# Dilated attention layer: rotary embedding moved from VectorE to GpSimd, and the first head's keys turned beside the memory queries

## What is computed

```python
DIL_GROUPS = ((128, 1), (512, 4), (2048, 16))
DIL_HEADS, DIL_HEAD_DIM, ROPE_DIM = 6, 128, 32

def partial_rope(x, pos):            # the first 32 of a head's 128 features
    half = ROPE_DIM // 2
    ...
    x1, x2 = xr[..., :half], xr[..., half:]
    rot = jnp.concatenate([x1 * cos - x2 * sin, x1 * sin + x2 * cos], axis=-1)
    return jnp.concatenate([rot, x[..., ROPE_DIM:]], axis=-1)

def dilated_mixer(h, w_in):
    for g, (window, dil) in enumerate(DIL_GROUPS):
        qkv = (h @ w_in[:, base:base + 3 * MIXER_WIDTH]).reshape(B, T, 3, DIL_HEADS, DIL_HEAD_DIM)
        q = partial_rope(qkv[:, :, 0], pos)
        k = partial_rope(qkv[:, :, 1], pos)
        o, lse = dilated_group(q, k, qkv[:, :, 2], window, dil)
    ...
    rest = h @ w_in[:, len(DIL_GROUPS) * 3 * MIXER_WIDTH:]
    q_mem, gate = jnp.split(rest, [MEM_WIDTH], axis=-1)
```

## Time and profile before

| | us |
|---|---|
| median of 3 runs | 3156.7 (3155.58 to 3156.95) |
| the profiled execution | 3151.94 |
| its span in the trace | 3150.6 |
| PE busy | 2860.4 (91%) |
| DVE busy | 1624.0 (52%) |
| ACT busy | 1019.8 (32%) |
| POOL busy | 182.2 (6%) |

### The profile page before, as it was taken

How to read it: one execution, slowest core, us unless ns; L and a number is a source line. 1 busy time by engine, 2 the same in 40 slices (tenths; PEclk the granted TensorE clock), 3 DMA queues, 4 the chain that set the end, 5 groups by cost and what they waited for, 6 DMA issues and landing times.

```text
span 3150.6 us, 43505 instructions
## 1 busy us (share of the span) xinstructions
PE 2860.4 (91%) x18290; PEld 2322.3 (74%) x18290; DVE 1624.0 (52%) x3099; ACT 1019.8 (32%) x1974; POOL 182.2 (6%) x258
## 2 busy tenths in 40 slices
PE   8988879999999988899699999999899897899998
PEld 6767667877776666688567888888666686578886
DVE  4333535544436455767864424343935677654444
ACT  3223422222234245343243212122425444332222
POOL 0000000000000000100000000000201244000001
PEclk9999989999999999899899999999999898899999
DMA  6433332232222210223522121121121110223231
GB/s 231 160 109 136 108 86 50 70 79 61 66 107 94 62 34 1 71 80 97 175 80 94 41 81 59 62 67 54 54 59 34 33 39 1 94 94 111 90 106 55
DMA packets 228878, 250.95 MB, mean 80 GB/s; under 512 B 6048, under 2 KB 193548, under 8 KB 227404
## 3 DMA queue, kind: packets, MB, share of 16 engines
q1 hardware_dynamic: 227008, 243.87, 24.4%
q0 software_dynamic: 1344, 4.20, 0.6%
q10 hardware_dynamic: 332, 0.12, 0.0%
HBM read 234.53 MB, written 9.44 MB: 77 GB/s over the span
## 4 chain that ended last, share of the span: by engine, by line
PE 68%; DVE 12%; ACT 4%; issue 2%; DMA 1%; POOL 0%; SPq 0%; DVEq 0%; ACTq 0%; POOLq 0%
PE PS L2235 63%; PE PS L2239 3%; ACT AR L182 1%; ACT L177 1%; DMA WR<-in_w_in 1%; PE PS L2424 1%; PE PS L2446 1%; DVE AR L3227 1%; DVE STAT L3159 1%; DVE AR L3066 1%; ACT EX L182 1%; DVE AR L3064 0%; DVE EX L3214 0%; DVE AR L2962 0%; ACT STAT L182 0%
## 5 line engine op out<-in xcount | busy, mean ns | idle before, releaser
L2235 PE MATMUL PS<-HI,WC 128*128 128x512 f32 (+2 forms) x1600 | 428.0, 353 | 0.7 <-DVE WC L3208 0.7
L2235 PE MATMUL PS<-AR 128*64 128x64 f32 (+7 forms) x3436 | 305.2, 269 | 64.0 <-ACT AR L182 27.2
L2235 PEld LDWEIGHTS PS<-AR 128*64 128x64 f32 (+5 forms) x3436 | 258.5, 171 | 116.4 <-issue 37.2
L182 ACT ACTIVATE AR<-PS 128x512 f32<-128x512 f32 (+5 forms) x353 | 152.1, 457 | 545.0 <-PE PS L2235 410.6
L2235 PEld LDWEIGHTS PS<-HI,WC 128*128 128x128 f32 x1600 | 284.0, 189 | 42.5 <-DVE WC L3208 1.1
L2235 PE MATMUL PS<-LO,WC 128*128 128x512 f32 (+2 forms) x800 | 282.2, 353 | 0.0
L2235 PE MATMUL PS<-HT,WR 128*128 128x256 f32 (+1 forms) x928 | 260.9, 434 | 6.0 <-DMA WR<-in_w_in 2.6
L2235 PE MATMUL PS<-WR,HT 128*128 128x128 f32 (+2 forms) x1296 | 251.6, 352 | 12.0 <-ACT AR L182 5.0
L182 ACT ACTIVATE EX<-PS 128x256 f32<-128x256 f32 (+2 forms) x158 | 66.6, 430 | 532.6 <-PE PS L2235 532.5
L2235 PEld LDWEIGHTS PS<-WR,HT 128*128 128x128 f32 x1296 | 191.7, 197 | 62.7 <-issue 39.1
L2235 PE MATMUL PS<-WC,AC 128*128 128x512 f32 x960 | 227.1, 393 | 0.3
(11 more groups left out here) (461 smaller groups left out, 5173.0 us busy)
## 6 DMA issues: line engine op xcount, KB each, us to landing
WR<-in_w_ffn_in SPq DMA_DIRECT2D x40, 1024.0 KB, 7.1
WR<-in_w_in_b SPq DMA_DIRECT2D x51, 512.0 KB, 6.8
WR<-in_w_mod SPq DMA_DIRECT2D x12, 2048.0 KB, 7.9
WR<-in_w_mod SPq DMA_DIRECT2D x24, 1024.0 KB, 5.6
WR<-in_w_ffn_out SPq DMA_DIRECT2D x22, 1024.0 KB, 4.9
WR<-in_w_in SPq DMA_DIRECT2D x40, 512.0 KB, 5.2
WR<-in_w_out SPq DMA_DIRECT2D x8, 2048.0 KB, 10.8
WR<-in_w_in SPq DMA_DIRECT2D x4, 2048.0 KB, 7.9
```

Source lines behind the costliest of these rows:

```text
L182: return self.o.activation(out, in_, func, **kw)
L2235: mm = lambda o, l, r, start, stop: e.o.matmul(o, l, r, start=start, stop=stop, skip_group_check=True)
```

## The change

All three operations of the rotary step go from DVE to POOL (`rope_d` becomes `rope_g`, with the same waits and the same semaphore), for all 12 steps. `rope_s` stays on POOL. For head 0 the keys' `rope_s` is still added at the end of `head_project(0)`, but their `rope_g` is held over in `owed_rope` and added in `memory_queries()`, after the work of f = 0; `qk_done[0]` is set there. Heads 1 to 5 keep their places in the plan.

```diff
         def memory_queries():
             owed_made()
             w = parts[3]
             parts_load(4, spill_done)
+            late, made = owed_rope[0]
...
                 for j in (2 * f, 2 * f + 1):
                     parts_made(4, j)
+                if f == 0:
+                    made += rope(*late)
+                    qk_done[0] = latest(made)
...
         def rope(x, copied):
 
-            if P.count["rope_s"] == P.count["rope_d"]:
+            if P.count["rope_s"] == P.count["rope_g"]:
                 P.add("rope_s", x, copied)
                 return []
-            return [("rope_d", 2 * P.add("rope_d", x, copied))]
+            return [("rope_d", 2 * P.add("rope_g", x, copied))]
...
-            for _ in late:
-                done += rope(*late)
+            if h == 0:
+                rope(*late)
+                owed_rope.append((late, done))
+                return
             qk_done[h] = latest(done)
```

More of the change, by code:

```diff
@@ L1361, in more_parts @@
                 high_made(p, step - 3)
-        owed_parts = []
+        owed_parts, owed_rope = [], []
         def owed_made():
@@ L3056, in rope @@
                 tt(x2, r4[2], r4[3], ALU.add).then_inc(sem(name))
[L3058 to L3068, removed]
             def rope_a(n, sg, rt, i, ready, until):
@@ L3229, in dve_program @@
             return dict(setup=setup, setup2=setup2, fence=fence, norm1=norm1, norm2=norm2, pj1=pj1, pjc=pjc, ma_x=ma_x, ma_t=ma_t, ma_f=ma_f, ga=ga, turn=turn_, mod_0=mod_0, mod_d=mod_d,
-                        gl=gl, hp1=hp1, hp2=hp2, hp5=hp5, hl1=hl1, hl2=hl2, hl4=hl4, hoe=hoe, rj=rj, gz=gz, g1=g1, g2=g2, g4=g4, g5=g5, g7=g7, rope_d=rope_d, rope_a=rope_a, qturn=qturn,
+                        gl=gl, hp1=hp1, hp2=hp2, hp5=hp5, hl1=hl1, hl2=hl2, hl4=hl4, hoe=hoe, rj=rj, gz=gz, g1=g1, g2=g2, g4=g4, g5=g5, g7=g7, rope_a=rope_a, qturn=qturn,
                         da_x=da_x, da_t=da_t, da_o=da_o, fnorm=fnorm, rr_c=rr_c, rg=rg, rr=rr, cols=cols, an=an, rs=rs, df_x=df_x, df_w=df_w, df_o=df_o, df_q=df_q,
@@ L3289, in rope_s @@
                     e.o.dma_start(w[lo:lo + 16, :, :], x[16 - lo:32 - lo, :, :]).then_inc(sem("rope_dm"), 16)
+            def rope_g(n, x, copied):
+                u, w = (a[0:32, :].rearrange("p (g n) -> p g n", g=3) for a in RTs)
+                cc, ss = (RC[0:32, 512 * c:512 * c + 512].unsqueeze(1).broadcast_to([32, 3, 512]) for c in range(2))
+                e.wait_all(copied)
+                e.wait_ge("tables", 80)
+                e.wait_ge("rope_d", 2 * n - 2)
+                tt(u, x, cc, ALU.mult)
+                e.wait_ge("rope_dm", 32 * n)
+                tt(w, w, ss, ALU.mult).then_inc(sem("rope_d"))
+                e.wait_ge("rope_d", 2 * n - 1)
+                tt(x, u, w, ALU.add).then_inc(sem("rope_d"))
             def swap(n, to, src, need):
@@ L3293, in swap @@
                 e.o.dma_start(to, src).then_inc(sem("swap"), 16)
-            return dict(fence=fence, swap=swap, rope_s=rope_s, hp2=hp2, hl1=hl1, hl2=hl2, g2=g2, an=an, dump=dumped(e))
+            return dict(fence=fence, swap=swap, rope_s=rope_s, rope_g=rope_g, hp2=hp2, hl1=hl1, hl2=hl2, g2=g2, an=an, dump=dumped(e))
         def sp_program(e):
```

## The result

The changed kernel takes 3128.7 us (median of 4 runs, 3127.2 to 3130.2) against 3156.1 of before: 27.4 us less, a ratio of 0.991 (95% interval 0.9899 to 0.9922). The forecast was 3137.0 us, 19.7 less, with a range of 3124 to 3151. The direction and the range held; the gain is 7.7 us larger than the sum.

What follows compares the result with a forecast made beforehand. PE, busy 91% of the span, bounds the kernel, so only its waits pay. Gains of 9.2, 5.0, 2.5 and 3 us sum to 19.7, from 3156.7 to 3137.0 us; range 3124 to 3151.

Steps and rivals of the forecast that it cites:

- the front: Between head 0 and the scores: head-0 keys leave DVE's queue, PE starts the memory queries earlier; 9.2 us, bounds 7 to 10.8.
- the held scaling: Ahead of the memory queries: the first scaling L2808 waits for POOL's first product, until 441.85 us, and ends at 442.6.
- The hold: Wherever POOL runs a product: a DVE operation that uses SBUF twice over waits until that product is done.
- Cover: Time before the scores need the turned keys, hiding POOL's slower step: 14 us for head 0, 17 us for head 1.
- The keys' steps: Five rotary steps of keys, heads 1 to 5, moved to POOL: net gain 1.0 us each, 5.0 us in all.
- The queries' steps: Five rotary steps of queries, heads 1 to 5: two PE waits of 1.27 us each go, 2.5 us.
- The clock: After three keys' steps the clock falls to 1.2 GHz for some 7 us; one such dip booked as gone, 3 us.
- the first rival, Everything comes through: Whole kernel: low parts slip between POOL's operations, all waits and clock dips go; 35 us, 3122 us, chance 0.14.
- Only the front pays: In the attention rounds held low parts cancel what is freed; only 9.2 us before the memory queries, 3147.5 us, chance 0.20.
- The hold-up eats the front too: Ahead of the memory queries PE starts 3.5 us later than forecast, rounds lose a little; 2 to 5 us gained, chance 0.08.
- Slower: POOL's product takes 6.9 us and holds low parts in each keys' step; 12.5 to 25 us lost, chance 0.08.

Runs made afterwards that it cites:

- e4: The changed kernel with GpSimd's first product put behind the wait for its DMAs, so all three products run in a row; 3126.6 us against 3157.6 of before.
- e6: The changed kernel with GpSimd's first product made three times in a row in each step; 3165.9 us against 3159.2 of before.
- e9: The changed kernel with the queries' rotary steps of heads 1 to 5 back on VectorE; 3135.9 us against 3159.2 of before.
- e1: The kernel before, all rotary products still on VectorE, only head 0's keys' step placed later in its queue; 3146.1 us against 3157.6 of before.
- e3: The changed kernel with head 0's two rotary steps back on VectorE in their old place, heads 1 to 5 on GpSimd; 3141.4 us against 3157.6 of before.
- e5: The changed kernel with GpSimd's three products cut to one element per group and partition, leaving out nearly all rotation; 3123.9 us against 3157.6 of before.
- e7: The changed kernel with the first keys' step added at its old place in the plan, engine still GpSimd; 3133.3 us against 3159.2 of before.
- e8: The changed kernel with GpSimd's first product behind the DMA wait, except for head 0's queries; 3122.8 us against 3159.2 of before.

## Why the prediction was right, and its sum too small

- **What bounds the kernel, and the front.** Forecast 9.2 us off a wait of 17.32; measured 9.4. The steps held as well: the product was put at 3.45 us, it takes 3.42 to 3.51, and up to 3.73 behind a low part; the held scaling at 3.2 us, it took 3.19. The hold is seen in e4, e6 and the changed kernel alike. The Trainium skill calls the port pair that the two engines share an exclusive lock ("SBUF — State Buffer", section "Who interferes with whom"), and the traces agree, with 3.19 us for 0.75 in the changed kernel and 7.51 us for 1.3 in e4.
- **Which operations are held.** "A DVE operation that uses SBUF twice over waits" was too wide. The row maximum reads SBUF and writes SBUF and was not held (below). It did no harm to the sum, which let only scalings and low parts wait.
- **Cover.** Put at 14 and 17 us. Head 0's keys end 12.8 us before their scores, head 1's 14.2 us; POOL never holds PE.
- **The keys' steps.** Forecast 5.0. At the first of them the shift of PE's matmuls is 1.5 us at the old wait less 0.7 at the new one for a low part, 0.8 against my 1.0. I then took that 1.0 for the other four. By the same reading they gave 1.3, 1.2, 2.0 and 0.9: 6.2 for the five. The rows with waits of 2.16, 2.40 and 3.64 said that they would give more.
- **The queries' steps.** Forecast 2.5; the shifts at their two waits are 1.3 and 1.4, and a further 0.7 us came at the wait at 669.9 of before, which I had not tied to a step and which e9 shows to go with one: 3.4.
- **The clock.** This is the term of the sum that failed most: one dip of three was booked, 3 us; all three went. By the shift of the starts they were worth 2.3, 2.8 and 2.3 us; what the keys' and queries' steps leave of the 16.8 us of the rounds is 7.2. So 4.2 of the 6.3 us by which the rounds beat my sum are here, 1.2 in the keys' and 0.9 in the queries' steps. e1 shows that the dips stay as long as DVE has the step. e3, e4 and e9 keep two short ones of 3.4 us each, e3 at the same waits as the changed kernel and e4 at fewer; e5, e7 and e8 keep none. How much of the clock's term a kernel gets is thus settled only as "most of it".
- **The rivals.** The measured time stands just past the edge of the forecast's own range (3129 to 3144), a good half of the way from the sum to the first rival; it is the wider range that held it. *Everything comes through* (35 us) was right that all dips go, though they were worth 7 us where it had 10.5. It was wrong on the mechanism: the low parts do not slip through, they are held in each key step. e8, which moves the hold away, comes near it, with 30.9 us in the stretch. *Only the front pays* fell with e3. *The hold-up eats the front too* fell with the changed kernel's wait of 7.89 us, and e6 shows what it would look like. *Slower* was rightly tied to POOL's time; with 6.9 us more to a step, e6 is 6.7 us slower than before, where I had 12.5 and more. It was not the same edit, as its long product is three short ones.
- **What I did not see.** DVE's last two low parts before the keys' end met the queries' third product in the changed kernel too, without harm. The same meeting cost e4 its front.

## What to carry to other kernels

Look at what stands behind a slow step in its queue before asking what the step costs: moving one that nobody needs yet from a shared queue to an idle engine gave 27 us here, though it doubles the step's time. The place alone counts too: in e1 a later one in the same queue gave 11.5 us. When GpSimd takes over work, place its products where VectorE has no operation with two operands in SBUF and no long scaling from SBUF to SBUF; here that was worth another 4 to 5 us in the stretch, for one wait moved by a line. A chain of short waits can also cost clock: here the stretches at 1.2 GHz behind three of them were worth some 7 us, against 10 of waits, and went with them.

## What the runs showed of the hardware

The hold doesn't depend on size: what DVE's operation loses is what is left of POOL's product. In e6 the pair on 8 elements took 3.45 us instead of 0.23, since POOL's product had begun 0.39 us ahead of it. Between two of POOL's products DVE gets one operation in (7.51 and 7.72 us for pairs of 1.3). Copies, masks and scalings that read PSUM ran at their length inside the products in all kernels here, and so did the row maximum, a reduction that reads one SBUF operand. This one, in the changed kernel, lies wholly inside the product of 519.53 to 523.03 and takes 1.49 us, as it does outside of one:

```profile
520.14 1.49 DVE L3088 TENSOR_REDUCE STAT<-AR 128x1 f32<-128x1280 f32 x1
```

The same busy time came with either level of the granted clock. This is the window of the changed kernel around the string of waits of the earlier trace rows. PE is busy 5.53 us of 7 in it, as it was in before, but the clock is 1.00 where it was 0.51:

```profile
523.00:530.00 7.00, 5.53 (x36) 4.72 (x36) 1.28 (x3) 2.30 (x6) 3.44 (x2) 1.00 0.01 2
```

At full clock PE got through 36 matmuls there, where it had 21 in as long a time at half clock. In the 7 us ahead of these windows PE had been busy 5.51 us in before (529:536) and 6.46 in the changed kernel (516:523).

The waits alone do not settle it either. At this place e4, e5 and e8 have the same two waits, 0.78 and 0.69 us, and no other; e4 has 3.4 us at 1.2 GHz there, e5 and e8 none. What tips it was not tried on its own.
